# Expert gathers of a hybrid decoder layer: key and value rows side by side, weights stored in the blocks that are read

## The reference

```
z = rmsnorm(h, g_norm) @ w_in                    # queries, keys, values, gates, convolution channels
h = h + [ rms(attention) ; rms(short conv) ] @ w_out
n = rmsnorm(h, g2)
qh = (n @ wq).reshape(tokens, 8, 2, 128)         # PEER: 8 heads
s  = einsum("trhk,hnk->trhn", qh, sub_keys)      # 128 sub-keys per side
sv, si = top_k(s, 16)                            # 16 + 16 halves, 256 pairs, the best 16 pairs
eidx = ...                                       # 16 experts per head: 128 experts per token
g   = softmax(fv)
act = gelu(einsum("td,trkd->trk", n, u_tab[eidx]))       # one dot product of 2048 per expert
h   = h + einsum("trk,trkd->td", g * act, v_tab[eidx])   # weighted sum of the value rows
y   = h + sigmoid(rmsnorm(h, g3) @ w_gate) * (p @ w_ple)
```

## Time and profile before

| | |
|---|---|
| runs | 2517.51, 2522.54, 2529.15 us |
| profiled execution | span 2524.0 us, first to last instruction; the page gives no time beyond it |
| PE busy | 1685.6 us (67%) |
| DVE busy | 1161.0 us (46%) |
| POOL busy | 913.2 us (36%) |
| ACT busy | 320.3 us (13%) |
| moved by DMA | 908.75 MB, 360 GB/s over the span |
| share of the chain that ended last | DMA 48%, PE 40% |
| DVE reduce of a u tile (L1530) | x320, 2292 ns each |
| POOL start of a u gather, of a v gather | x320 each, 1754 ns and 1099 ns |

### The profile page before, as it was taken

How to read it: one execution, slowest core, us unless ns; L and a number is a source line. 1 busy time by engine, 2 the same in 40 slices (tenths; PEclk the granted TensorE clock), 3 DMA queues, 4 the chain that set the end, 5 groups by cost and what they waited for, 6 DMA issues and landing times.

```text
span 2524.0 us, 21534 instructions
## 1 busy us (share of the span) xinstructions
PE 1685.6 (67%) x8372; PEld 917.0 (36%) x8372; DVE 1161.0 (46%) x2146; ACT 320.3 (13%) x705; POOL 913.2 (36%) x644
## 2 busy tenths in 40 slices
PE   8999989997997649688788332233333223577778
PEld 3445665696775337433376000000000000122224
DVE  2010322134455763544533666565565765644433
ACT  0000221010002322200200100101001012101002
POOL 0000000012234443422533556565666665645440
PEclk9998997998998776599699666656666665778799
DMA  9943483779999997999999999999999999999998
GB/s 358 333 164 123 125 315 107 268 254 411 366 399 375 369 379 301 391 382 373 400 411 360 418 418 422 421 421 421 422 421 421 421 421 418 402 416 416 416 415 325
DMA packets 215844, 908.75 MB, mean 360 GB/s; under 512 B 17350, under 2 KB 40879, under 8 KB 131808
## 3 DMA queue, kind: packets, MB, share of 16 engines
q0 software_dynamic: 92160, 671.13, 64.4%
q1 hardware_dynamic: 123126, 235.36, 26.3%
q10 hardware_dynamic: 458, 0.91, 0.1%
HBM read 895.31 MB, written 14.53 MB: 360 GB/s over the span
## 4 chain that ended last, share of the span: by engine, by line
DMA 48%; PE 40%; DVE 4%; POOL 3%; issue 3%; ACT 2%; SPq 0%; ACTq 0%; DVEq 0%; PEldq 0%; POOLq 0%
DMA arena<-in_peer_v,arena 31%; PE bank L1747 9%; PE bank L2182 5%; DMA arena<-in_w_in 5%; PE bank L2197 5%; DMA arena<-in_peer_u,arena 4%; DMA arena<-in_peer_wq 3%; DMA arena<-in_w_out 3%; PE bank L1821 3%; PE bank L1958 2%; PE bank L1934 2%; PE bank L2306 2%; PE bank L2131 2%; POOL arena L669 2%; PE bank L2108 1%
## 5 line engine op out<-in xcount | busy, mean ns | idle before, releaser
L1530 DVE CUSTOM_DVE_ANT_0 arena<-arena 128x2048 f32<-128x2048 f32 x320 | 730.7, 2292 | 581.5 <-DMA arena<-in_peer_u,arena 578.1
L2182 PE MATMUL bank<-arena 128*32 128x512 f32 x2560 | 459.9, 823 | 672.7 <-DVE arena L1539 539.1
L669 POOL DMA_INDIRECT arena<-in_peer_u,arena x320 | 561.2, 1754 | 860.6 <-DVEq L1509 566.4
L674 POOL DMA_INDIRECT arena<-in_peer_v,arena x320 | 351.7, 1099 | 689.6 <-PE bank L2182 663.2
L2182 PEld LDWEIGHTS bank<-arena 128*32 128x32 f32 x2560 | 67.1, 127 | 1003.7 <-DVE arena L1539 522.6
L1747 PE MATMUL bank<-arena 128*128 128x512 f32 (+2 forms) x544 | 216.3, 558 | 5.4 <-PE bank L1747 4.1
L2197 PE MATMUL bank<-arena 128*128 128x192 f32 x1024 | 189.9, 348 | 24.4 <-DMA arena<-in_w_in 23.2
L2197 PEld LDWEIGHTS bank<-arena 128*128 128x128 f32 x1024 | 181.5, 205 | 45.6 <-DMA arena<-in_w_in 28.5
L1747 PEld LDWEIGHTS bank<-arena 128*128 128x128 f32 (+1 forms) x544 | 101.4, 208 | 116.7 <-issue 116.4
L2306 PE MATMUL bank<-arena 128*128 128x512 f32 x256 | 125.6, 650 | 0.0
L986 ACT ACTIVATE arena<-arena 128x4 f32<-128x4 f32 x80 | 16.8, 210 | 849.6 <-DVE arena L1530 849.4
(11 more groups left out here) (270 smaller groups left out, 1490.5 us busy)
## 6 DMA issues: line engine op xcount, KB each, us to landing
arena<-in_w_in SPq DMA_DIRECT2D x22, 2048.0 KB, 9.4
arena<-in_w_in SPq DMA_DIRECT2D x32, 1024.0 KB, 14.6
arena<-in_w_out SPq DMA_DIRECT2D x8, 2048.0 KB, 9.7
arena<-in_peer_wq SPq DMA_DIRECT2D x8, 2048.0 KB, 8.1
arena<-in_w_out SPq DMA_DIRECT2D x16, 1024.0 KB, 16.3
arena<-in_peer_wq SPq DMA_DIRECT2D x16, 1024.0 KB, 23.0
arena<-in_ple_gate SPq DMA_DIRECT2D x32, 512.0 KB, 15.4
arena<-in_ple_gate SPq DMA_DIRECT2D x6, 2048.0 KB, 13.3
```

What stands on the lines that cost most here:

```text
L669: pool.indirect_dma_start(u_row[j], None, I["peer_u"][0], bass.IndirectOffsetOnAxis(idx[:, i, c + j:c + j + 1], 0)).then_inc(u_in[j], 16)
L674: pool.indirect_dma_start(v_row[j], None, I["peer_v"][0], bass.IndirectOffsetOnAxis(idx[:, i, c + j:c + j + 1], 0)).then_inc(v_in[j], 16)
L1530: dve.tensor_tensor_reduce(out=u_row[j], in0=u_row[j], in1=rep_of(i), scale=1.0, scalar=0.0, op0=ALU.mult, op1=ALU.add, accum_out=a4[:, pa ...
L2182: ins = pe.matmul(bank[i % 2][32 * q:32 * q + 32, :], diag[:, k % 2, j, :], v_row[j][:, 512 * q:512 * q + 512], start=(s == 0 and j == 0), ...
```

## The change

It has three parts.

1. **Layout of the weights.** w_in, w_out, peer_wq, ple_gate and ple_proj are handed over as blocks (block, partition, k, 512 columns), cmp_w1 as (kind, d, m, h). What one fill reads for one partition is then one contiguous piece: 16 KB for a fill of 2 MB, 8 KB for one of 1 MB, 4 KB for one of 0.5 MB, instead of 2 KB pieces; for cmp_w1 12 and 20 KB instead of 1 KB. The SBUF side was contiguous before. The order and the number of the fills stay.
2. **One table of experts.** Row e of `experts` is u_tab[e] followed by v_tab[e], 16 KB. SBUF has four tiles of 128 x 4096 in the place of the eight; `u_row[j]` and `v_row[j]` are the halves of one tile. One gather fetches both, so there are 320 gathers of 2 MB for 640 of 1 MB. A gather waits for `v_used` alone: u's half is no longer free when DVE has read it.
3. **Each tile weighed alone.** ACT takes the gelu of one column at a time, DVE builds the diagonal matrix of that tile by one instruction (line 1553 of the changed kernel, for the two before), and PE waits for that matrix alone. DVE's order becomes reduce, diagonal, reduce, diagonal, with `between` behind the last.

With it come two small moves. ACT's square root in step 66 now stands behind the gelu. The first fill of the tail waits for `v_used` of all but two tiles, where it waited for the last `u_used`.

```diff
-    u_row = [buf(W0 + j * D, D) for j in range(4)]
-    v_row = [buf(W0 + (4 + j) * D, D) for j in range(4)]
+    uv_row = [buf(W0 + 2 * j * D, 2 * D) for j in range(4)]
+    u_row, v_row = [a[:, 0:D] for a in uv_row], [a[:, D:2 * D] for a in uv_row]
...
-                fill(2 * blk + half, w_view["in"][:, 8 * half:8 * half + 8, c0:c0 + n], n)
+                fill(2 * blk + half, w_piece("in", c0, 8 * half, 8), n)
...
             if i == 1:
-                sp.wait_ge(u_used, 4 * STEPS)
+                sp.wait_ge(v_used, 4 * STEPS - 2)
...
             for j in range(4):
                 if k:
-                    pool.wait_ge(u_used, 4 * (k - 1) + j + 1)
-                pool.indirect_dma_start(u_row[j], None, I["peer_u"][0],
-                                        bass.IndirectOffsetOnAxis(idx[:, i, c + j:c + j + 1], 0)).then_inc(u_in[j], 16)
-            for j in range(4):
-                if k:
                     pool.wait_ge(v_used, 4 * (k - 1) + j + 1)
-                pool.indirect_dma_start(v_row[j], None, I["peer_v"][0],
-                                        bass.IndirectOffsetOnAxis(idx[:, i, c + j:c + j + 1], 0)).then_inc(v_in[j], 16)
+                pool.indirect_dma_start(uv_row[j], None, I["experts"],
+                                        bass.IndirectOffsetOnAxis(idx[:, i, c + j:c + j + 1], 0)).then_inc(uv_in[j], 16)
...
         def gelu(k):
-            act.wait_ge(u_used, 4 * k + 4)
-            act.activation(w4[:, k % 2, :], a4[:, k % 2, :], ACT.Gelu_apprx_tanh).then_inc(gelu_done, 1)
+            for j in range(4):
+                act.wait_ge(u_used, 4 * k + j + 1)
+                act.activation(w4[:, k % 2, j:j + 1], a4[:, k % 2, j:j + 1], ACT.Gelu_apprx_tanh).then_inc(gelu_done, 1)
...
             for j in range(4):
-                dve.wait_ge(u_in[j], (k + 1) * 16)
+                dve.wait_ge(uv_in[j], (k + 1) * 16)
                 dve.tensor_tensor_reduce(out=u_row[j], in0=u_row[j], in1=rep_of(i), scale=1.0, scalar=0.0,
                                          op0=ALU.mult, op1=ALU.add, accum_out=a4[:, par, j:j + 1]).then_inc(u_used, 1)
+                if k >= 2:
+                    dve.wait_ge(v_used, 4 * (k - 2) + j + 1)
+                dve.wait_ge(gelu_done, 4 * k + j + 1)
+                dve.scalar_tensor_tensor(out=diag[:, par, j, :], in0=sel, scalar=w4[:, par, j:j + 1],
+                                         in1=rep(wgt[:, i, c + j:c + j + 1], [0, 32]), op0=ALU.mult, op1=ALU.mult)\
+                   .then_inc(diag_ready, 1)
             if between:
                 between()
-            if k >= 2:
-                dve.wait_ge(v_used, 4 * (k - 1))
-            dve.wait_ge(gelu_done, k + 1)
-            dve.tensor_tensor(w4[:, par, :], w4[:, par, :], wgt[:, i, c:c + 4], ALU.mult).then_inc(weighed, 1)
-            dve.wait_ge(weighed, k + 1)
-            dve.tensor_tensor(diag[:, par], rep(sel, [0, 4], [1, 32]), rep(w4[:, par, :], [1, 4], [0, 32]), ALU.mult)\
-               .then_inc(diag_ready, 1)
...
-                pe.wait_ge(diag_ready, k + 1)
-            pe.wait_ge(v_in[j], 16 * (k + 1))
+            pe.wait_ge(diag_ready, 4 * k + j + 1)
```

## The result

The changed kernel takes 2564.7 us (median of four runs, 2562.62 to 2566.79), the kernel before 2523.45 us beside it (2517.51 to 2529.15): ratio 1.0163, 95% interval 1.0141 to 1.0185. That is 41 us slower. Forecast were 2520 us, within 2478 to 2562. Both profiled executions show it: spans of 2563.3 and 2524.0 us.

A forecast was written before the change was run, and what follows sets the result against it. PE bounds the kernel up to 560 us, then DMA, through inefficient transfers or engines holding them back. Terms -11 - 8 - 6 + 14 - 4 + 13 = -2 on 2524.0, less 1.5 for the median: about 2520 us, range 2478 to 2562.

The forecast's parts named there:

- second rival: Four tiles run dry: late gelu before three reduces, PE releases late, DMA idles; +38, 2561 us, chance 0.25.
- the two signs that the forecast named for being wrong: DMA share under 0.98 in steps 28 to 63, or 798 to 1065 us taking less time than before.
- Steps 8 to 11 are the other way round: Prompt attention: PE begins behind the first reduce instead of the fourth, worth 3 us once.
- The late waits of steps 13 to 15: Sample attention: three more reduces behind ACT's late gelu, before DVE's item; +4, +4.5 and +8.5.
- The whole stage: 798 to 1065 us: late-gelu delays less the gain of steps 8 to 11; +14, bounds 0 and +30.
- The reserve of 4.7 us: Steps 28 to 63: a slot's round sums to 14.9 us of a 19.6 us cycle, so holding tiles costs 0.
- +6 in step 21 alone: 1065 to 1384 us: the second norm waits for DVE's item; +6.
- -8 - 6 - 10 = -24: Blocks: transfer rate -8 and w_in's larger share -6 from 560 to 798 us, rate -10 from 1065 to 1384.
- The fourth rival: 560 to 798 us: queue shares stay unchanged, so the -6 goes; sum +4, 2526 us, chance 0.06.
- two new waits: From 1065 us on: they use up any share gain of the weights; +6 in step 21, stage total -4.
- Forecast -11 for steps 28 to 63: Gathers alone: half as many descriptors save 0.3 us a step over 36.8 steps; -11, bounds -20 to +10.
- Forecast +13: Gates and tail: +3 for each of three cycles, +3 for step 66, +1 for the tail; bounds 0 and +30.

The follow-up runs named there:

- experiment 1: Kernel before with only the weights in blocks; separate 8 KB gathers and weighing all at once as before: 2488.14 us, ratio 0.9867.
- experiment 5: Changed kernel without its table: blocks and each tile weighed alone, but u and v gathered apart into eight tiles: 2527.9 us, ratio 1.0007.
- Experiment 9: Kernel with blocks and whole rows, each tile weighed alone, in steps 32 to 63 only (2480 us), changed to do so from step 16 on: 2499.85 us.

## Why the prediction was wrong

The forecast was no change, 2520 us; the change costs 41. Its second rival, with a chance of 0.25, had 2561 us, almost the number. That it came so near is luck: it had +28 for the sample stage, +4 for the next and +25 for the gates, where +44.8, -3.1 and +10.7 came. And its mechanism, four tiles that run dry, is only a part of it: in steps 7 to 16 the weighing costs 42.7 us with eight tiles too. Neither of the two signs that the forecast named for being wrong was met: the DMA share from 1384 to 2116 us is 0.98, and the sample stage became longer, not shorter.

**The step that failed: "Steps 8 to 11 are the other way round: PE begins behind the first reduce instead of the fourth, which is worth 3 us once".** It was costed at -3. Experiments 1 and 5 put these steps at +26. The error was one of reading. In steps 8 to 11 DVE waited 0.35 us for the gelu, so ACT was taken to be in time. But the wait stood behind four reduces. A wait that moves forward by three reduces is not to be judged by its idle time in the old trace, but by when ACT is free, against the new place. That could have been worked out: ACT free at 7.2 us, 0.5 for the gelu and the hand-over, then 8.5 for three more reduces with theirs is 16.2 us, where DVE had taken 9.2 + 0.35; so +6.6 in step 8, and likewise +4.7, +3.4 and +6.6 in the others. The sum is +21, near the +26; step by step it fits less well (+1.6, +9.6, +5.0 and +10.1 by the two runs), since a delay in one step moves the items of the next. That reason is argued, not shown. The late waits of steps 13 to 15 were in view, and their sum (17) was, if anything, too high: steps 12 to 16 lost 11.5 by the same two runs, and step 7, for which there was no term, 5.0.

**The whole stage.** Forecast +14, measured +44.8. Of it +42.7 is the weighing with eight tiles, +13.7 the table on top, and -11.6 the blocks, which were counted at nothing there.

**The reserve of 4.7 us.** It was enough in steps 32 to 63, where DMA was never short of work (share 1.01). But the sum was trusted where PE is behind an item. Experiment 9 puts that at +18.0 for steps 17 to 27, where the forecast had +6 in step 21 alone.

**The blocks.** Forecast -8 - 6 - 10 = -24; experiment 1 gives -35 by the medians, -39 by the spans (+3.3 up to step 0, -12.1 in steps 0 to 6, -11.6 in 7 to 16, -20.6 in 17 to 27, +1.8 in the rest). The sign and the mechanism were right: as many packets of one queue as of the other, 767 beside 774, and a third of the bytes for w_in. The Trainium skill, DMA: Bandwidth & Descriptors, section on queues, rings and completion order, has whole packets of several descriptors drained from one ring. The fourth rival took from it that the shares would stay. They didn't: w_in went from 21% of the bytes to 34%, which refutes that rival. The equal counts alone don't refute the page's rule, which would give them too if the packets of both rings had as many descriptors. The size was off: "nothing from 1065 on, where two new waits use it up" mixed two parts of the change. It looked right in the end, with -4 forecast and -3.1 measured, but that is luck: the blocks' part was put at -10 and came at -20.6, the two new waits at +6 and came at +19.3.

**The gathers.** Forecast -11 for steps 28 to 63, measured -6.8: -10.0 in steps 32 to 63 (-11.5 from the table itself), and 3.2 lost in steps 28 to 31: the first gather of step 32 waits for DVE's indices (POOL's timeline),

```profile
1499.94 0.94 POOL L691 DMA_INDIRECT arena<-in_experts,arena  x1 [18.90 <-DVEq L1527]
```

and from 1490 to 1500 us the DMA share is 0.20. With eight tiles POOL waits there too (13.56 us in the kernel before, to 1462.93), but the tiles already under way keep the DMA share at 1.01.

**Gates and tail.** Forecast +13, measured +9.8 and +0.9. From one block of four quarters on PE to the next it was to be 74 us:

```profile
2275.05 15.19 PE L2322 MATMUL bank<-arena 128*128 128x512 f32 x32
2293.56 1.07 PE L2198 MATMUL bank<-arena 128*32 128x512 f32 x8 [3.32 <-DVE arena L1553]
...
2351.24 14.64 PE L2322 MATMUL bank<-arena 128*128 128x512 f32 x32
```

It is 76.2, and the first tile starts 3.3 us behind the block (the earlier trace rows and the forecast's 3.2).

**Up to step 0** the forecast had no term and 7.7 us came. Two parts show. PE's first instruction came at 12.9 in place of 9.88, and the first gather starts 3.1 us later (556.46 for 553.34). That gather has 2 MB, and DVE used it 10.9 us after its issue, where 1 MB took 6.2: 4.6 us more.

Of the 13.7 us that four tiles cost in steps 7 to 16, 7.5 lie at step 16 (46.8 us for the 39.4 of experiment 5), which ends with POOL's stop of 40.3 us. What the other 6 are is open.

## What to carry to other kernels

A wait that shows next to no time in a trace may stand in the shadow of the work ahead of it; before moving it forward, take away that work's time and read when the releaser is done. Two changes that delay the same chain need not add: in steps 7 to 16 they cost 43 and 41 us by themselves and 56 together, so undoing one looked like little. And a change with parts of different sign is worth cutting by stage: the blocks everywhere and whole rows in 32 of 80 steps gave 2480 us, where all parts everywhere gave 2565.

## What the runs showed of the hardware

- Where both queues have work, they move as many packets as each other, with rows of 16 KB beside pieces of 8 KB too (767 and 774 in 40 us). So weights read in small pieces beside long gathered rows get few bytes: beside rows of 8 KB, PE's waits for them were 53.5 us with 2 KB pieces, 1.2 with 8 KB.
- Long pieces work against small loads: with 16 KB pieces in flight the gain rows that PE's first instruction needs came 3.3 us later than with pieces of 2 KB.
- A row of 16 KB took 623 engine-ns (0.622 x 16 x 2563.3 us over 40,960 rows, with their semaphore writes), two of 8 KB 635 (from the earlier trace rows): 12 ns per row saved. In whole stages it was 0.35 us a step of 32 rows per engine, so 11 ns.
- A gather's start on POOL took 0.93 to 1.07 us where DVE was idle, and up to 3.06 us where DVE was busy: 534.1 us for 320 starts here, 912.9 for 640 before.
- PE's granted clock over steps 32 to 63 was 0.62 with the tiles weighed at once, 0.58 with each weighed alone in eight tiles (experiment 5), and 0.50, that is 1.2 GHz throughout, in the kernel after. At 1700 us the kernel before did a step's four tiles within 8 us and then paused for 12; the kernel after did one tile every 4.9 us, with pauses of 2.6 to 3.5. A tile took 1.94 to 1.98 us at that clock, and 1.06 at full clock. It is 0.9 us more in a slot's round, where the reserve was enough for it.
